# A hybrid attention, linear attention and MoE layer on one core: chunks of the linear attention in pairs, Silu on ScalarE, bias table written 128 times and read back skewed

## The reference

```python
rel = kpos[None, :] - qpos[:, None]
bias = rel_bias[t5_bucket(rel)].transpose(2, 0, 1)
s = jnp.einsum('bhmqd,bhmkd->bhmqk', qblk, kt) + bias[None, :, None]
...
def step(state, inp):                      # per chunk of 64, in order
    ...
    k_dec = kn * jnp.exp(total - cum)
    state = jnp.exp(total[:, :, 0])[..., None] * state + jnp.einsum('bhcd,bhce->bhde', k_dec, vn)
    return state, jnp.einsum('bhcd,bhde->bhce', qn, state)
...
ob = rms_norm(ob, g_norm_b).reshape(Bn, S, B_WIDTH) * jax.nn.silu(rb)
return jnp.concatenate([oa, ob], axis=-1) @ w_out
```

## Time and profile before

| | |
|---|---|
| median of 3 runs | 1503.46 us (1501.86 to 1504.16) |
| span of the profiled execution | 1501.0 us |
| PE busy | 1246.9 us (83%) |
| VectorE busy | 772.2 us (51%) |
| ScalarE busy | 207.4 us (14%) |
| GpSimd busy | 45.4 us (3%) |
| moved by DMA | 581.93 MB, mean 388 GB/s |
| chain that ended last | PE 38%, DMA 35%, SP's queue 16%, VectorE 9% |

### The profile page before, as it was taken

One profiled execution on the slowest core, in us unless ns is written; L12 is line 12 of the kernel. 1 busy time (PEld: TensorE's weight loads), 2 busy tenths in 40 slices (PEclk: granted clock), 3 DMA queues, 4 the chain that ended last, 5 costly groups with the idle time before them and its releaser, 6 DMA issues.

```text
span 1501.0 us, 19016 instructions
## 1 busy us (share of the span) xinstructions
PE 1246.9 (83%) x7349; PEld 552.2 (37%) x7350; DVE 772.2 (51%) x1102; ACT 207.4 (14%) x477; POOL 45.4 (3%) x68
## 2 busy tenths in 40 slices
PE   4699999999999999976777767766776679999977
PEld 4588544744444443322222212212221223333322
DVE  5876257777688666534233323432342334555525
ACT  3011131221111032100000000000000001111103
POOL 0001200000000001000000000000000000000010
PEclk9899999999999999999789898988898989999989
DMA  9999979888789779999999999999999999999996
GB/s 354 393 383 385 368 261 361 307 337 304 295 321 382 306 292 395 427 423 426 428 426 424 428 426 425 425 429 426 425 427 427 426 425 428 426 426 425 427 426 262
DMA packets 101668, 581.93 MB, mean 388 GB/s; under 512 B 6680, under 2 KB 31536, under 8 KB 57856
## 3 DMA queue, kind: packets, MB, share of 16 engines
q1 hardware_dynamic: 98752, 572.81, 93.8%
q10 hardware_dynamic: 1664, 6.46, 1.1%
q0 software_dynamic: 1216, 2.17, 0.5%
HBM read 579.29 MB, written 2.13 MB: 387 GB/s over the span
## 4 chain that ended last, share of the span: by engine, by line
PE 38%; DMA 35%; SPq 16%; DVE 9%; issue 1%; ACT 1%; POOL 0%; ACTq 0%; DVEq 0%
DMA stream<-in_w 32%; PE ps L709 10%; PE ps L918 6%; PE ps L634 5%; SPq L546 5%; SPq L565 4%; SPq L540 4%; PE ps L972 3%; PE ps L791 3%; DMA stream<-in_w_ada 2%; DVE wk L1058 2%; PE ps L879 2%; PE ps L706 1%; PE ps L824 1%; PE ps L925 1%
## 5 line engine op out<-in xcount | busy, mean ns | idle before, releaser
L918 PE MATMUL ps<-stream,wk 128*32 128x512 f32 x2304 | 320.2, 683 | 135.7 <-DMA stream<-in_w 134.9
L1385 DVE TENSOR_TENSOR acc<-ps,acc 128x2048 f32<-128x2048 f32 x37 | 84.8, 2292 | 429.6 <-PE ps L879 429.6
L918 PEld LDWEIGHTS ps<-stream,wk 128*32 128x32 f32 x2304 | 70.6, 117 | 374.4 <-issue 296.6
L972 PE MATMUL ps<-stream,cst 128*32 128x512 f32 x1152 | 153.1, 660 | 61.8 <-DMA stream<-in_w 61.7
L709 PE MATMUL ps<-stream 128*128 128x512 f32 x448 | 199.2, 599 | 0.3 <-PE ps L634 0.3
L709 PEld LDWEIGHTS ps<-stream 128*128 128x128 f32 x448 | 83.9, 191 | 100.3 <-issue 99.6
L634 PE MATMUL ps<-stream 128*128 128x256 f32 x512 | 118.0, 394 | 1.8 <-ACT stream L1530 1.8
L634 PEld LDWEIGHTS ps<-stream 128*128 128x128 f32 x512 | 100.9, 198 | 16.7 <-issue 1.9
L925 PEld LDWEIGHTS ps<-cst,wk 128*128 128x128 f32 x576 | 70.2, 192 | 62.8 <-issue 62.8
L1058 DVE SCALAR_TENSOR_TENSOR wk<-stream,cc,wk 128x768 f32<-128x768 f32 (+1 forms) x90 | 83.6, 929 | 11.5 <-DMA stream<-in_w_ada 8.9
L879 PE MATMUL ps<-wk,cst 32*128 32x512 f32 x592 | 88.3, 668 | 0.8 <-ACT wk L1701 0.8
(11 more groups left out here) (275 smaller groups left out, 1015.5 us busy)
## 6 DMA issues: line engine op xcount, KB each, us to landing
stream<-in_w SPq DMA_DIRECT2D x190, 2048.0 KB, 40.8
stream<-in_w_ada SPq DMA_DIRECT2D x64, 1024.0 KB, 6.0
stream<-in_w_in SPq DMA_DIRECT2D x8, 4096.0 KB, 16.7
stream<-in_w_ada SPq DMA_DIRECT2D x64, 384.0 KB, 10.0
stream<-in_w_out SPq DMA_DIRECT2D x4, 4096.0 KB, 15.3
stream<-in_w_ada SPq DMA_DIRECT2D x16, 512.0 KB, 10.2
stream<-in_w_in SPq DMA_DIRECT2D x4, 2048.0 KB, 13.7
stream<-in_w_in SPq DMA_DIRECT2D x2, 3072.0 KB, 16.2
```

Source lines behind the costliest of these rows:

```text
L918: last = nc.tensor.matmul(bank(1 + m)[32 * g:32 * g + 32, :], xe[:, k + g, :], w13[m][:, k + g, :], start=(k == 0), stop=(k == KD - 4))
L972: last = nc.tensor.matmul(bank(2)[32 * g:32 * g + 32, :], hid[:, k, :], w2v[:, k, 512 * g:512 * g + 512], start=(k == 0), stop=(k == 3))
L1385: V.tensor_tensor(y4, ps[:, b0:b0 + 4, :], y4, ALU.add).then_inc(ysum_sb, 1)
```

## The change

Three things are changed.

- Two chunks, those of one tile of 128 positions, are handled in one item. `kv` issues for each head the matmul of the lower chunk and that of the upper one (rows 0 to 63 and 64 to 127 of the array), into four banks; VectorE computes both states one behind the other, into two buffers; `glao` issues the two chunks' outputs alternately (columns 0 to 63 and 64 to 127). The items stand in slots 25 to 27; `gsq`, `gmul` stand in other slots.
- The items `silu` are gone. ScalarE's copy out of PSUM of the units 10 and 11 applies Silu instead.
- The eight rows of the bias are written to DRAM 128 times each, so that reading with a stride of one less than a row gives each partition its row shifted the right way round. The `flip` on PE and ScalarE is gone. The write has 8 x 128 rows of 1536 B where it had 8; the read has 1024 rows of 1024 B in both.

```diff
@@ schedule()
-    beside[5].append(("flip",))
...
-    for j in range(5):
-        if j:
-            beside[25 + j].append(("glao", j - 1))
-        if j < 4:
-            beside[25 + j].append(("kv", j))
-    beside[26] += [("silu", 0, 0)]
-    beside[28] += [("gsq", 0), ("silu", 1, 0)]
-    beside[29] += [("gmul", 0, 0)]
-    beside[30] += [("gsq", 1), ("silu", 0, 1), ("gmul", 0, 1)]
-    beside[31] += [("gmul", 1, 0), ("glaT", 0)]
+    beside[25].append(("kv", 0))
+    beside[26] += [("glao", 0), ("kv", 1)]
+    beside[27] += [("glao", 1), ("gsq", 0)]
+    beside[28] += [("gsq", 1)]
+    beside[29] += [("gmul", 0, 0), ("gmul", 1, 0)]
+    beside[30] += [("gmul", 0, 1)]
+    beside[31] += [("glaT", 0)]
...
-            out += [("silu", 1, 1), ("gmul", 1, 1), ("partial", 4), ("wout", 0, 0), ("glaT", 1), ("mod", 4)]
+            out += [("gmul", 1, 1), ("partial", 4), ("wout", 0, 0), ("glaT", 1), ("mod", 4)]
@@ build()
-        kdec, state = view(gl, 0, TT, 512), view(gl, 1024, B_HEADS, B_DV)
+        kdec, states = view(gl, 0, TT, 512), [view(gl, 1024 * (1 + i), B_HEADS, B_DV) for i in range(2)]
...
+        def kv_of(i, h):
+            return bank(6 - 2 * i + h // 2, 2, B_DV)[:, h % 2, :]
...
-        reldram = dram("reldram", [A_HEADS, SKEW])
+        reldram = dram("reldram", [A_HEADS, P, SKEW])
@@ tensor
-                        pe.wait_ge(gla_sb, 2)
+                        pe.wait_ge(gla_sb, 3)
...
-                elif kind == "flip":
-                    pe.wait_ge(bias_in, 16)
-                    for j in range(4):
-                        if j == 3:
-                            pe.wait_ge(flip_sb, 1)
-                        nc.tensor.matmul(bank((2, 3, 6)[j % 3]), cst[:, C_FLIP:C_FLIP + P], wk[:, 512 * j:512 * j + 512], start=True, stop=True).then_inc(flip_ps, 1)
...
-                            pe.wait_ge(flip_sb, 4)
...
                 elif kind == "kv":
-                    n = item[1]
-                    t, lo = n // 2, CHUNK * (n % 2)
-                    if n == 0:
+                    t = item[1]
+                    if t == 0:
...
+                    else:
+                        pe.wait_ge(state_sb, 4)
                     for h in range(B_HEADS):
-                        last = nc.tensor.matmul(bank(6 + h // 2, 2, B_DV)[:, h % 2, :], kdec[lo:lo + CHUNK, t, P * h:P * h + P],
-                                                vb[lo:lo + CHUNK, t, B_DV * h:B_DV * h + B_DV], start=True, stop=True)
+                        for i in range(2):
+                            lo = CHUNK * i
+                            last = nc.tensor.matmul(kv_of(i, h), kdec[lo:lo + CHUNK, t, P * h:P * h + P],
+                                                    vb[lo:lo + CHUNK, t, B_DV * h:B_DV * h + B_DV], start=True, stop=True)
                     last.then_inc(kv_ps, 1)
                 elif kind == "glao":
-                    n = item[1]
-                    t, lo = n // 2, CHUNK * (n % 2)
-                    pe.wait_ge(state_sb, n + 1)
+                    t = item[1]
+                    pe.wait_ge(state_sb, 4 * t + 4)
                     for h in range(B_HEADS):
-                        last = nc.tensor.matmul(bank(2 + 2 * t + h // 2, 2, B_DV)[lo:lo + CHUNK, h % 2, :], qbT[:, h, CHUNK * n:CHUNK * n + CHUNK],
-                                                state[:, h, :], start=True, stop=True)
+                        for i in range(2):
+                            lo, n = CHUNK * i, 2 * t + i
+                            last = nc.tensor.matmul(bank(2 + 2 * t + h // 2, 2, B_DV)[lo:lo + CHUNK, h % 2, :], qbT[:, h, CHUNK * n:CHUNK * n + CHUNK],
+                                                    states[i][:, h, :], start=True, stop=True)
                     last.then_inc(gla_ps, 1)
...
-                    pe.wait_ge(gla_sb, 2 * t + 2)
+                    pe.wait_ge(gla_sb, 3 + t)
@@ vector
-                elif kind == "silu":
...
-                    dve.wait_ge(rb_exp, 2 * c + t + 1)
-                    link(V.tensor_scalar_add(e, e, 1.0))
-                    link(V.reciprocal(e, e))
-                    V.tensor_tensor(r, r, e, ALU.mult).then_inc(rb_sb, 1)
                 elif kind == "kv":
...
+                    t = item[1]
+                    dve.wait_ge(kv_ps, t + 1)
+                    for i in range(2):
+                        n = 2 * t + i
+                        if i:
+                            dve.wait_ge(state_sb, 4 * t + 2)
+                        elif t:
+                            dve.wait_ge(gla_ps, 1)
+                        for h in range(B_HEADS):
+                            if n == 0:
+                                ins = V.tensor_copy(states[0][:, h, :], kv_of(0, h))
+                            else:
+                                ins = V.scalar_tensor_tensor(out=states[i][:, h, :], in0=states[1 - i][:, h, :], scalar=st[:, DECAY(n, h):DECAY(n, h) + 1],
+                                                             in1=kv_of(i, h), op0=ALU.mult, op1=ALU.add)
+                        ins.then_inc(state_sb, 2)
...
-                    dve.wait_ge(rb_sb, 2 * c + t + 1)
+                    dve.wait_ge(proj_sb, FILLS - 4 + 2 * c + t + 1)
@@ scalar
-                elif kind == "flip":
-                    for j in range(4):
-                        act.wait_ge(flip_ps, j + 1)
-                        A(wk[:, 512 * j:512 * j + 512], bank((2, 3, 6)[j % 3]), ACT.Copy).then_inc(flip_sb, 1)
...
-                    A(dst, src, ACT.Copy, scale=scale).then_inc(proj_sb, 1)
+                    A(dst, src, ACT.Silu if c >= 10 else ACT.Copy, scale=scale).then_inc(proj_sb, 1)
...
-                elif kind == "silu":
...
-                    A(tmp[:, 512 * t:512 * t + 512], rb[:, t, 512 * c:512 * c + 512], ACT.Exp, scale=-1.0).then_inc(rb_exp, 1)
...
-                    act.wait_ge(gla_ps, 2 * t + 2)
+                    act.wait_ge(gla_ps, t + 1)
@@ gpsimd
-            pool.dma_start(reldram[:, :], relrow).then_inc(rel_out, 16)
+            pool.dma_start(reldram[:, :, :], relrow.unsqueeze(1).to_broadcast((A_HEADS, P, SKEW))).then_inc(rel_out, 16)
             pool.wait_ge(rel_out, 16)
-            pool.dma_start(bias, bass.AP(tensor=reldram[:, :].tensor, offset=0, ap=[[1, P], [SKEW, A_HEADS], [1, S]])).then_inc(bias_in, 16)
+            pool.dma_start(bias, bass.AP(tensor=reldram[:, :, :].tensor, offset=P - 1, ap=[[SKEW - 1, P], [SKEW * P, A_HEADS], [1, S]])).then_inc(bias_in, 16)
...
-            pool.wait_ge(flip_sb, 4)
+            pool.wait_ge(bias_in, 16)
```

More of the change, by code:

```diff
@@ L374, in build @@
         wr_in, turned, part_sb, padded, diag_sb = sem("wr_in"), sem("turned"), sem("part_sb"), sem("padded"), sem("diag_sb")
-        flip_ps, flip_sb = sem("flip_ps"), sem("flip_sb")
         early_w_in = [sem(f"early_w_in{j}") for j in range(3)]
@@ L395, in build @@
         kv_ps, state_sb, gla_ps = sem("kv_ps"), sem("state_sb"), sem("gla_ps")
-        rb_exp, rb_sb, gla_sq, gla_rs, gla_sb = sem("rb_exp"), sem("rb_sb"), sem("gla_sq"), sem("gla_rs"), sem("gla_sb")
+        gla_sq, gla_rs, gla_sb = sem("gla_sq"), sem("gla_rs"), sem("gla_sb")
         glaT_ps, glaT_sb = sem("glaT_ps"), sem("glaT_sb")
@@ L1261, in _ @@
                                         ALU.mult).then_inc(oT_sb, 1)
-                elif kind == "silu":
-                    _, t, c = item
-                    r, e = rb[:, t, 512 * c:512 * c + 512], tmp[:, 512 * t:512 * t + 512]
-                    dve.wait_ge(rb_exp, 2 * c + t + 1)
-                    link(V.tensor_scalar_add(e, e, 1.0))
-                    link(V.reciprocal(e, e))
-                    V.tensor_tensor(r, r, e, ALU.mult).then_inc(rb_sb, 1)
-                elif kind == "kv":
-                    n = item[1]
-                    dve.wait_ge(kv_ps, n + 1)
-                    for h in range(B_HEADS):
-                        kv = bank(6 + h // 2, 2, B_DV)[:, h % 2, :]
-                        if n == 0:
-                            ins = V.tensor_copy(state[:, h, :], kv)
-                        else:
-                            ins = V.scalar_tensor_tensor(out=state[:, h, :], in0=state[:, h, :], scalar=st[:, DECAY(n, h):DECAY(n, h) + 1], in1=kv,
-                                                         op0=ALU.mult, op1=ALU.add)
-                    ins.then_inc(state_sb, 1)
-                    dve.wait_ge(state_sb, n + 1)
+                elif kind == "kv":
+                    t = item[1]
[13 more added lines that the diff above has]
+                        ins.then_inc(state_sb, 2)
                 elif kind == "gmul":
@@ L1619, in _ @@
                         act.wait_ge(o_sq, g + 1)
-                elif kind == "silu":
-                    _, t, c = item
-                    act.wait_ge(proj_sb, FILLS - 4 + 2 * c + t + 1)
-                    act.wait_ge(la_sb, 2)
-                    if c:
-                        act.wait_ge(rb_sb, t + 1)
```

(3 more changed lines are left out.)

## The result

The changed kernel takes 1508.21 us (median of 5 runs, 1505.64 to 1510.39) where the kernel before takes 1503.46: a ratio of 1.0035, 95% interval 1.0023 to 1.0046. It is slower, by a little; the forecast was 1492.6 us, 15.6 us less than measured. The profiled execution spans 1503.8 us.

A forecast was written before the change was run, and what follows sets the result against it. PE was taken to bound the kernel up to about 580 us, then the experts' weight stream. 8.0 + 0.8 + 0.4 + 1.7 = 10.9 us off 1503.46 gave 1492.6 us; the range was 1489 to 1499.5 us.

The forecast's parts named there:

- Pairs: Linear attention on PE: paired chunks overlap by two in the array, four blocks cost 8.0 us, saving 8.0 us.
- Silu: Gated output: without reciprocals PE's 0.8 us wait goes, and the second output product moves up by 0.4 us.
- The table loads: ScalarE: two extra loads, before the first Silu and the routing's Exp; at most 0.1 us shows, 1.5 by the skill.
- The flip: First attention block: PE loses 3.43 us but waits for VectorE's probabilities, so 1.7 us arrive.
- The clock: PE's clock after waits: 1.9 us may be lost at 229.4 us and 1.9 regained at the second output product.
- The bias table: Bias write to DRAM grows to 1.57 MB, takes 8.2 us on eight engines, and costs nothing.
- the cover: Bias write: some 38 us may pass before VectorE wants the bias; past that each microsecond is lost.
- Rival (d): Bias write crawls out of 8 partitions, 65 us on one engine, bias late by 26.5 us: 1519 us; chance 0.06.
- Rival (b): Fourth modulation's fold: VectorE starves as ada loads queue behind a 4 MB load, 4.3 us lost: 1496.9 us; chance 0.10.

The follow-up runs named there:

- experiment 10: Kernel before with the chunks in pairs alone, `gsq` and `gmul` in the changed kernel's slots; exp, reciprocal, small write and flip stay: 1501.01 us, ratio 0.9991.
- experiment 4: Changed kernel, but PE makes 16 copies of each head's row on 128 partitions, each written 8 times: 1492.25 us, ratio 0.9931.
- experiment 8: Changed kernel with bias rows written from 128 partitions and the first attention item ahead of its slot's ada steps: 1488.6 us, ratio 0.9902.
- experiment 1: Changed kernel with the old bias path, the 12 KB write and the flip, put back: 1491.13 us, ratio 0.9925.
- Experiment 3: Changed kernel with the 12 KB write and flip put back, plus a 1.57 MB write that no engine reads: 1509.51 us, ratio 1.0042.
- Experiment 12: Changed kernel with its eight source rows on partitions 0, 4, 8 to 28, each written 128 times: 1492.47 us, ratio 0.993.

## Why the prediction was wrong

**Pairs: right.** 16 instructions of 256 columns in 2.00 us, four blocks 7.90 us: both halves overlap by two, as the earlier trace rows had it for other matmuls. From the first block to the four slots at 421.65 us after are 21.74 us, less two slots of 6.87: 8.0 us, for 16.04.

**Silu: right in its size, but not a term of its own.** Alone it shortens the stretch by 1.3 us, and with the pairs by what makes their 8.0 up to 9.2, both as forecast. Without it, though, the pairs' 8.0 us go in the wait for VectorE's gated product and the half clock behind it (experiment 10). That product stands behind an ada load and a reciprocal; what each adds wasn't tested apart. The prediction asked whether VectorE keeps up only with Silu in place, which was the right question for the whole change, but its terms can't be taken singly. The table loads: two more stand in the trace, 1.28 us each, and the routing shows 0.2 us of them at most, where 0.1 was forecast; the 1.5 us that the prediction set beside it didn't come (the way from the second output product to the experts' first expansion is 575.37 - 463.70 - 1.69 = 109.98 us before, and 578.62 - 468.42 = 110.20 after).

**The flip: right in the waits, and worth nothing.** This is a second term that failed, a smaller one: 1.7 us were forecast, and with the write made fast (experiment 4) the stretch was 0.84 us longer than with the flip. PE waited 1.97 us at the first probabilities where 1.7 were forecast, and 0.41 ahead of it. What was left over went to the clock, 1.7 us; with the wait gone (experiment 8) taking the flip away is worth 3.34.

**The clock: right by its sum, and by luck.** The two places were set against each other at 1.9 us each. In experiment 4 each came out, at 1.7: one given back behind the 1.80 us wait at 454 us, one taken behind 1.97 us at 231. But the length of the wait didn't decide it. The changed kernel and experiment 1 have the same attention wait of 1.80 us; behind it the slot took 7.03 us in the one (at 368.99) and in the other

```profile
353.61 0.44 PE L745 MATMUL ps<-cst,wk 128*128 128x128 f32 x2 [1.80 <-DVE wk L1254]
353.89 8.73 PE L710 MATMUL ps<-stream 128*128 128x512 f32 x16
```

There it made no difference to the end: with the slot at full clock PE met a further wait of 1.59 us for VectorE (at 378.05), which experiment 1 doesn't have. What decides whether the clock falls isn't settled here.

**The bias table: this is the step that failed.** "I cost it at nothing; the cover is some 38 us for the write alone, and past that each microsecond is lost." The write took 35.9 us, inside that cover, and cost 15.2 us of stretch all the same. The step had two faults. The size: 8.2 us, from 24 GB/s for an engine, came from loads that spread over all 128 partitions. Eight rows in neighbouring partitions gave 4608 bytes in 715 ns, 6.4 GB/s an engine, and 35.9 us. The meaning: the cover of 38 us was asked for the bias's sake only, and there it all but held (the mask ended at 228.36, wanted at 228.1). The engines that the write holds are also those of every load on SP's queue, whose next loads, a 4 MB unit and the ada quarters, VectorE and then PE wait for. Experiment 3 shows that with a write that nobody needs: +15.6 us of stretch. From experiment 1 to the changed kernel the sum closes: waits of 15.39 and 1.67 us, 8.37 instead of 7.03 us for the slot behind them, 0.80 instead of 0.49 for the scores, less the flip's 3.43: 15.3 us, where the stretches differ by 304.66 - 289.44 = 15.2. (Behind that the two kernels differ by the wait of 1.59 us and the slot of 8.73 us above, which cancel.)

Rival (d) had the crawl, and its reason (all rows come out of 8 partitions), but priced it as lateness of the bias, decided it from 38 us on, and gave it 0.06. Rival (b) had the starving of VectorE behind a 4 MB load, at another place and from another cause. The two together are what happened, and the prediction didn't join them.

**Why the source is slow.** 178 ns for a packet is 4608 / 178 = 26 GB/s for an engine. 361 is twice that, 715 four times. A single division explains all rows with a source in SBUF: partitions 0 to 3 share one way out, 4 to 7 the next, and engines on one way share its 26 GB/s. Then partitions 0 to 7 are two ways with four engines on each (4 x 178 = 712 ns), and 0, 16 to 112 would be four ways with two each if partitions 32 apart share one (64 apart would give the same 361 ns; no run tells the two apart). Experiment 12 puts one engine on each of eight ways and finds 178. The spare write alone moved 50 GB/s, two ways' worth. The Trainium skill (SBUF — State Buffer, Door 1: The DMA port swizzle) has this as 16 ports, each for four neighbouring partitions and the four 32 above them, at about 27 GB/s; by it the eight rows reach two ports, and 1.57 MB would take an estimated 29 us. The traces agree as to the groups of four and the rate: 35.9 us, of which some 5 us are what the small write of 12 KB took too. The pairing with the four 32 above is only consistent with them. The rule speaks against this change, and the prediction didn't weigh it. Sixteen rows on 0 to 15 are four ways with four engines each: 712 ns by this, the median is 438 and the upper tenth at 718. The engines didn't all run at one time: in the first 4 us fewer than nine packets were under way on average, with a median of 178 ns, from the eighth to the twelfth 12.7, with 694; the landing (1.57 MB by 104 GB/s is 15.1 us, and 4 to 5 us of latency) fits its 19.2.

## What to carry to other kernels

Price a DMA by both its ends, and count the ways out of the memory on its SBUF side, not only its engines: eight rows in neighbouring partitions, repeated by a stride of zero, came out at 50 GB/s here; spread the rows (every fourth partition was enough) or let PE make the copies. Then ask not only when the transfer's own reader needs it, but which other queue's loads use the same engines meanwhile, and who waits for those: a slow packet holds its engine all the longer (half of the engines for 50 GB/s in experiment 3). And where two parts of a change work on one chain, one on PE and one on the engine that feeds it, time them together and apart; here the two gave 9.2 us of stretch together, and 1.4 and 1.3 apart.

## What the runs showed of the hardware

- The time of a packet out of SBUF depended on where the source's partitions lay, over a factor of four: 715, 361 and 178 ns for the same 4608 bytes, from eight partitions in all three, with some eight packets under way at once. The landing changed by less, 35.9, 20.4 and 17.6 us.
- A DMA share of 0.50 and 50 GB/s can stand in one line of the stretch table: the share tells how long engines are held, not that they move much. Eight rows held half of the sixteen engines.
- The PE wait of 1.80 us ahead of the second output product was followed by full clock (41.47 us) wherever it stood; in the kernel before and with the new bias path alone the product took 43.16 us. At 231 us a wait of 1.97 us was followed by a slot of 8.73 us instead of 7.03. Behind one and the same attention wait of 3.1 us the slot took 7.07 us (experiment 10), 7.38 (changed kernel), 8.38 (kernel before) and 8.74 (experiment 1). In the changed kernel the clock had fallen to half by the end of the wait of 15.39 us:

```profile
235.00:240.00 5.00, 0.00 (x0) 0.00 (x0) 0.00 (x0) 0.00 (x0) 0.00 (x0) 0.50 1.01 413
```

- The start of PE's first slot moved between 163.8 and 167.7 us from one profile to another.
